# w_out and five more projections by seven products of quarters, and a first layer that begins in five parts

## The reference, cut to what matters

```
# first block, one layer (p: its weights)
shift, scale, gate = split(silu(c) @ p.w_ada + p.b_ada)      # same for ctx with c_ctx
h = x * (1 + scale) + shift                                  # ctx likewise
(a_q, a_k, a_v, a_g, g_q, g_k, g_v, g_af, g_ab, g_g,
 s_u, s_v, s_g, m_a, m_g, m_s) = split(h @ p.w_in)
y_attn = attention(a_q, a_k, a_v) * silu(a_g)
y_gla  = rms(gla scan, both directions) * silu(g_g)
y_sgu  = s_u * (w_s mixed over tokens of layer_norm(s_v) + b_s) * silu(s_g)
m   = sigmoid(m_a) * (y_attn @ w_br_attn) + sigmoid(m_g) * (y_gla @ w_br_gla) + sigmoid(m_s) * (y_sgu @ w_br_sgu)
x   = layer_norm(ALPHA * x + gate * (m @ w_out))             # ctx too, in the first layer only
# second block, one layer
h = rms(x) * norm_w ;  y = sigmoid(g0) * y_a + sigmoid(g1) * y_b ;  x = x + y @ w_out
# end
out = rms(x) * final_norm_w
```

## Time and profile before

| | us |
|---|---|
| median of three runs | 1534.58 |
| the profiled execution, whole | 1532.09 |
| its span (first to last instruction) | 1530.3 |
| PE busy | 1491.9 (97%) |
| DVE busy | 755.5 (49%) |
| ACT busy | 429.2 (28%) |
| POOL busy | 287.6 (19%) |

### The profile page before, as it was taken

The page is one execution under the profiler, slowest core; times in us unless marked ns, Lnnn a source line. Parts: engine busy times, 40 slices in busy tenths (PEclk is TensorE's granted clock), DMA queues, the critical chain, the costliest instruction groups (busy, mean ns, idle before and its releaser), DMA issues.

```text
span 1530.3 us, 20417 instructions
## 1 busy us (share of the span) xinstructions
PE 1491.9 (97%) x8416; PEld 1123.3 (73%) x8416; DVE 755.5 (49%) x1546; ACT 429.2 (28%) x846; POOL 287.6 (19%) x314
## 2 busy tenths in 40 slices
PE   6999999999999999999999999999999999999997
PEld 2577776554788884655977988588888858888883
DVE  1266656642634333533745631356887215679621
ACT  1132454323121220122336330134333213423310
POOL 0223203200566441122111202110100011010010
PEclk9999999999999999999999999999999999999999
DMA  9542224300122213421332352533232233232221
GB/s 370 225 165 111 111 110 166 135 31 20 63 96 106 100 57 102 152 110 55 110 111 110 111 221 110 195 115 121 111 112 106 109 150 145 110 129 99 105 110 42
DMA packets 17376, 184.31 MB, mean 120 GB/s; under 512 B 2306, under 2 KB 2818, under 8 KB 4740
## 3 DMA queue, kind: packets, MB, share of 16 engines
q1 hardware_dynamic: 17284, 183.01, 31.3%
HBM read 181.95 MB, written 1.05 MB: 120 GB/s over the span
## 4 chain that ended last, share of the span: by engine, by line
PE 89%; ACT 3%; DVE 3%; issue 2%; DMA 2%; POOL 1%; SPq 0%; POOLq 0%; ACTq 0%; DVEq 0%
PE ps L850 85%; PE ps L905 3%; DVE arena L1933 2%; DMA arena<-in_wf 2%; POOL arena L2607 1%; DVE arena L1927 0%; ACT L1887 0%; ACT L1885 0%; ACT arena L1459 0%; DVE arena L2134 0%; DVE arena L1930 0%; ACT arena L1885 0%; ACT arena L1771 0%; ACT L1773 0%; ACT L1771 0%
## 5 line engine op out<-in xcount | busy, mean ns | idle before, releaser
L850 PE MATMUL ps<-arena 128*128 128x256 f32 (+9 forms) x7924 | 1443.6, 365 | 28.1 <-DMA arena<-in_wf 13.5
L850 PEld LDWEIGHTS ps<-arena 128*128 128x128 f32 (+5 forms) x7924 | 1070.2, 178 | 368.7 <-issue 236.4
L2607 POOL TENSOR_TENSOR arena<-arena 128x256 f32<-128x256 f32 (+6 forms) x254 | 254.5, 1021 | 808.9 <-DVE arena L1933 374.2
L1933 DVE SCALAR_TENSOR_TENSOR arena<-arena 128x256 f32<-128x256 f32 (+4 forms) x482 | 237.8, 544 | 115.1 <-ACT arena L1486 21.2
L1459 ACT ACTIVATE arena<-ps 128x512 f32<-128x512 f32 (+3 forms) x312 | 148.9, 499 | 485.7 <-PE ps L850 410.6
L1927 DVE TENSOR_TENSOR arena<-arena 128x1024 f32<-128x1024 f32 (+12 forms) x253 | 205.8, 838 | 150.8 <-ACT arena L1459 83.2
L1927 DVE TENSOR_TENSOR arena<-ps,arena 128x512 f32<-128x512 f32 (+16 forms) x141 | 59.9, 449 | 123.8 <-PE ps L850 115.3
L1933 DVE SCALAR_TENSOR_TENSOR arena<-arena,ps 128x256 f32<-128x256 f32 (+2 forms) x109 | 47.2, 445 | 132.6 <-PE ps L850 90.7
L905 PEld LDWEIGHTS ps<-arena 128*128 128x128 f32 x488 | 55.8, 141 | 28.2 <-issue 18.3
L905 PE MATMUL ps<-arena 128*128 128x128 f32 x488 | 72.2, 278 | 1.3 <-DVE arena L1927 0.7
L1933 DVE SCALAR_TENSOR_TENSOR arena<-ps,arena 128x128 f32<-128x128 f32 (+2 forms) x86 | 30.8, 407 | 82.6 <-PE ps L850 82.2
(11 more groups left out here) (96 smaller groups left out, 308.2 us busy)
## 6 DMA issues: line engine op xcount, KB each, us to landing
arena<-in_wf SPq DMA_DIRECT2D x69, 2048.0 KB, 8.0
arena<-in_wf SPq DMA_DIRECT2D x22, 1024.0 KB, 7.8
arena<-in_wf SPq DMA_DIRECT2D x2, 1152.0 KB, 7.7
arena<-in_xinT SPq DMA_DIRECT2D x2, 1024.0 KB, 16.0
arena<-in_xin SPq DMA_DIRECT2D x4, 512.0 KB, 3.8
arena<-in_rp SPq DMA_DIRECT2D x2, 1024.0 KB, 8.4
arena<-in_consts SPq DMA_DIRECT2D x1, 1410.0 KB, 21.1
arena<-in_pa SPq DMA_DIRECT2D x2, 532.0 KB, 9.8
```

Of the source, the lines that this page charges most:

```text
L850: return e.matmul(o, l, r, start=start, stop=stop, skip_group_check=True)
L1933: return e.scalar_tensor_tensor(out=o, in0=x, scalar=s, in1=y, op0=op0, op1=op1)
L2607: return e.tensor_tensor(o, x, y, op)
```

## The change

- w_out of all four layers by seven products: four matmuls of 256 columns each, for a pair of token tiles and a half j of the outputs. A token tile is the stationary operand, the weight quarter moves. The two halves are interleaved (OUT_ORDER).
- VectorE makes the sums of w_out's weight quarters (8 of 128x1024 in each layer) during the last part of the merge, and the sums of the merged tokens (4 of 128x512 for each pair) after it. Product 1 of each half waits only for the first half of the features (`mg_add.at(l, 7)`, `mb_add.at(l, 3)`).
- sg and ma0 in both layers and mg1 in the second by seven products; sg now before su, and su is multiplied into the gated sg by VectorE (kind "M").
- Two buffers in turn (TM, TMB) for the addends of the merge, two for zz.
- The first layer begins in five parts: parts n carry k chunks (1, 1, 2, 2, 2) of shift and scale in one piece, and x transposed together with q's weights for those chunks; q is accumulated part by part. GpSimd makes no part of hT any more.
- The last norm is taken in quarters (squares) and halves (product and output).
- The order strings are other ones, and the pieces' places in the ring shift.

```diff
-ADA_FIRST = [(0, 0), (0, 2), (0, 1), (0, 3)]
+ADA_FIRST = [(0, 1), (1, 2), (2, 4), (4, 6), (6, 8)]
+OUT_PART = {1: (0, 0), 2: (0, 0), 6: (0, 1), 4: (0, 1), 7: (1, 1), 5: (1, 1), 3: (1, 0)}
+OUT_ORDER = [(0, 1), (0, 2), (0, 7), (0, 6), (1, 1), (0, 4), (1, 7), (1, 2), (1, 6), (1, 4), (0, 5), (1, 5), (0, 3), (1, 3)]
-SEVEN = [[("gqk", "A"), ("gv", "A"), ("ag", "T"), ("gg", "T"), ("su", "A")],
-         [("ag", "T"), ("gg", "T"), ("su", "A"), ("mg0", "G"), ("ms0", "G"), ("ma1", "G")]]
+SEVEN = [[("gqk", "A"), ("gv", "A"), ("ag", "T"), ("gg", "T"), ("sg", "T"), ("su", "M"), ("ma0", "G")],
+         [("ag", "T"), ("gg", "T"), ("sg", "T"), ("su", "M"), ("ma0", "G"), ("mg0", "G"), ("ms0", "G"), ("ma1", "G"),
+          ("mg1", "G")]]
-        short = [("a0gqk", "a0su"), ("a1ag", "a1ma1")]
+        short = [("a0gqk", "a0ma0"), ("a1ag", "a1mg1")]
-                    out[f"a{l}o{j}"] = ou_pe.at(l, NOUT[l] - 2 + j)
-                    out[f"b{l}o{j}"] = ob_pe.at(l, 2 + j)
+                    out[f"a{l}o{j}"] = a_out_made(l, len(PAIRS[l]) - 1, j, 4)
+                    out[f"b{l}o{j}"] = out_made(l, j, 4)
# SP, start
+            for n, (k0, k1) in enumerate(ADA_FIRST):
+                load(f"a0f{n}")
+                if n == 0:
+                    fetch(BADA[:, 0:24], pa[0][:, 0:24], d_bada)
+                    fetch(cst[:, C_ID:C_MASK], consts[:, C_ID:C_MASK], d_id)
+                fetch(FX[:, k0:k1, :], r3(first, 8)[:, k0:k1, :], d_first[n])
...
-            s.wait_ge(mg_dve.end(0), mg_add.end(0))
+            s.wait_ge(mg_pe.at(0, MGI[0][("m", "s", 1, 3)]))
# TensorE, start
-                    for n in range(2):
-                        ada_products(n, "pf", *ADA_FIRST[n])
...
+                    for n in range(len(ADA_FIRST)):
+                        first = (1, 2)[n == 2]
+                        for t in range(first if n else 0):
+                            first_queries(n - 1, t)
+                        ada_products(n, "pf", f"a0f{n}")
+                        for t in range(first, first + 1 if n else 0):
+                            first_queries(n - 1, t)
+                        ada_columns(n, "ps", "pf")
+                        for t in range(first + 1, 4 if n else 0):
+                            first_queries(n - 1, t)
# TensorE, w_out of layer_a (layer_b: out_product, the same with out_added, TO, WO)
-                p.wait_ge(mg_dve.end(l), mg_add.end(l))
-                for i, (t, hf) in enumerate((t, hf) for t in tiles(l) for hf in range(2)):
-                    token(bank("ou", l, i), use(f"a{l}o{hf}", 8), 512, mT, 128 * t).then_inc(ou_pe.hit(l, i), 1)
+                for pr in range(len(PAIRS[l])):
+                    for i, (j, x) in enumerate(OUT_ORDER):
+                        a_out_product(l, pr, j, x).then_inc(ou_pe.hit(l, 14 * pr + i), 1)
+            def a_out_product(l, pr, j, x):
+                ...
+                    b = psum("ou", l, pr, j, 7 if x == 4 else 1)
+                    p.wait_ge(a_out_taken(l, pr, j, {6: 1, 5: 6, 4: 7, 3: 5}[x]))
+                p.wait_ge(mg_add.at(l, 7) if x == 1 else mg_add.at(0, 14) if (l, pr, x) == (0, 0, 2) else mg_add.end(l))
+                ...
+                for k in range(4):
+                    ins = mm(b[:, 0:256], H[:, k, :], W[:, k, :], x in (1, 2, 7) and k == 0, k == 3)
# TensorE, layer_b
-                    if l == 0 and i == 3:
+                    if l == 0 and i == 13:
                         input_b(1, 0)
# ScalarE, layer_a
+                for pr in range(len(PAIRS[l])):
+                    for i, (j, x) in enumerate(BY_COPY):
+                        t, f = OUT_PART[x]
+                        a.wait_ge(a_out_made(l, pr, j, x), ln_x.at(l, t) if pr else None)
+                        o = SIG[1][:, 256 * j:256 * j + 256] if x == 7 else zz[t][:, 512 * j + 256 * f:512 * j + 256 * f + 256]
+                        copy(o, psum("ou", l, pr, j, 7 if x == 7 else 1)[:, 0:256]).then_inc(ou_act.hit(l, 8 * pr + i), 1)
# VectorE, layer_a: sums between the parts
+                            for _ in range((3, 3, 2, 0)[c] if l and (br, j) == ("s", 1) else 0):
+                                next(sums)
+                first = a_out_token_sums(l, 0)
+                next(first)
+                next(first)
+                sums = chain(first, sums, a_out_token_sums(l, 1) if l == 0 else ())
+                ...      # for each of OUT_ORDER: add, next(sums, None), after x in (4, 3) gated_half, after j = 1 normed
# VectorE, layer_b: a sum after each product of the last branch
-                for _ in merge(l, 1):
-                    pass
+                sums = out_weight_sums(l)
+                for n, _ in enumerate(merge(l, 1)):
+                    if n % 2:
+                        next(sums)
+            def out_weight_sums(l):
+                for j in range(2):
+                    w11, w12, w21, w22 = (quarter(weights(f"b{l}o{j}", 8), k, f) for f, k in ("11", "12", "21", "22"))
+                    v.wait_ge(pieces[f"b{l}o{j}"][2])
+                    tt(WO[j]["3"], w11, w21, ALU.subtract).then_inc(ob_w.hit(l, 4 * j), 1)
+                    yield
+                    ...      # 2 = w22 - 3, 1 = w21 + w22, 4 = w12 - 2
```

More of the change, by code:

```diff
@@ L1 @@
 from contextlib import ExitStack
+from itertools import chain
 import numpy as np
@@ L300, in build_program @@
         KDT = [attf[:, 0:512], attf[:, 512:1024]]
-        QB = [ma.take(512) for _ in range(2)]
+        qb = ma.take(1024)
+        QB = [qb[:, 0:512], qb[:, 512:1024]]
         ST = ma.take(1024).rearrange("p (d n v) -> p d n v", d=2, n=4)
@@ L2233, in later_piece @@
                     put(kind, 2, dst, 1, 1, MS_11 + o)
+                    if not o:
+                        next(sums, None)
+                        next(sums, None)
                     if o:
@@ new lines, in normed @@
+            def normed(l, pr, pair, t):
+                z, st, k, tile = zz[t], st6[:, 16 * t:16 * t + 16], pair[t] - tiles(l)[0], pair[t]
+                v.wait_ge(v.now())
+                e.bn_aggr(st[:, 12:14], r3(st[:, 0:12], 2)).then_inc(ln_st.hit(l, k), 1)
+                o = X[:, 1024 * t:1024 * t + 1024] if tile >= 2 else CX[:, 1024 * t:1024 * t + 1024]
+                v.wait_ge(ln_st.at(l, k), landed(d_rp, l))
+                stt(z, z, st[:, 12:13], rp[:, 0:1024], ALU.subtract, ALU.mult).then_inc(v.own(), 1)
+                v.wait_ge(v.now(), ln_rs.at(l, k))
+                stt(o, z, st[:, 14:15], rp[:, 1024:2048], ALU.mult, ALU.add).then_inc(ln_x.hit(l, k), 1)
@@ new lines, in layer_b @@
+                for n, _ in enumerate(merge(l, 1)):
+                    if n % 2:
+                        next(sums)
+                out_sums = out_token_sums(l)
+                next(out_sums)
+                next(out_sums)
+                for i, (j, x) in enumerate(OUT_ORDER):
+                    t, f = OUT_PART[x]
+                    o = X[:, 1024 * t + 512 * j + 256 * f:1024 * t + 512 * j + 256 * f + 256]
+                    v.wait_ge(ob_pe.at(l, i), out_added(l, j, {2: 1, 4: 6, 5: 7}[x]) if x in (2, 4, 5) else None)
+                    stt(o, psum("ou", 2 + l, j, {2: 2, 7: 7, 4: 7}.get(x, 1))[:, 0:256], 0.5, o, ALU.mult, ALU.add
+                        ).then_inc(ob_x.hit(l, i), 1)
+                    next(out_sums, None)
+                    if l and i in (10, 13):
+                        last_norm(i == 13)
@@ new lines, in last_norm @@
+            def last_norm(t):
+                ms = f2[:, 8 + t:9 + t]
+                v.wait_ge(fn_sq.at(1, 4 * t + 3))
+                e.tensor_reduce(ms, f2[:, 4 * t:4 * t + 4], AX, ALU.add).then_inc(v.own(), 1)
+                v.wait_ge(v.now())
+                ts(ms, ms, 1.0 / 1024, EPS, ALU.mult, ALU.add).then_inc(fn_ms.hit(1, t), 1)
+                v.wait_ge(fn_rs.at(1, t), landed(d_fr))
+                for hf in range(2):
+                    x = X[:, 1024 * t + 512 * hf:1024 * t + 512 * hf + 512]
+                    stt(x, x, ms, fr[:, 512 * hf:512 * hf + 512], ALU.mult, ALU.mult).then_inc(fn_x.hit(1, 2 * t + hf), 1)
@@ L2847 @@
     pieces = {}
+    for n, (a, b) in enumerate(ADA_FIRST):
+        w = I["w_ada"][0]
+        pieces[f"a0f{n}"] = lay(np.concatenate([w[:, o + 128 * a:o + 128 * b] for o in (0, 1024)], 1))
     for l in range(2):
```

518 lines of the change are left out of this document (319 added, 199 removed).

## The result

The changed kernel takes 1495.02 us, median of four runs (1493.66 to 1496.71), against 1534.36 (1532.9 to 1535.61; one run more than above): 0.975 of the time before, 95% interval 0.9735 to 0.9765. That is 39.3 us less where 33.7 was forecast (1501 from a range of 1493 to 1512). Measured again beside the first experiments it gave 1496.16 (1495.71 to 1497.12). The profiled execution took 1493.66, 38.4 less than the one before.

The account below looks back on a forecast made before the run. TensorE's work was taken as the bound, busy 1491.9 of 1530.3 us. Terms -28.2 -5.5 -5.4 +1.0 +3.3 -0.9 +2.0 = -33.7 gave a median of 1500.9, forecast 1501 us, range 1493 to 1512.

Parts of the forecast that it names:

- Products taken away: w_out, sg, ma0 and mg1 by seven products: fewer TensorE records, 28.2 us less.
- The start: Up to q's last copy: smaller parts let TensorE begin earlier, 5.5 us less, bounds 2 and 7.
- Seams from merge to w_out: Before each w_out: first product needs only half the features, covering the last addition; 5.4 of 5.8 us back.
- Inside w_out: First layer's w_out: TensorE waits for VectorE's late copy at the second pair, +1.0 us, bounds 0 and 4.
- Seam to the second block: Between the blocks: first token tile complete later and rp landing late, TensorE stands, +3.3 us, bounds 0 and 6.
- The end: After the last matmul: last norm in quarters and halves, write half as large, 0.9 us less.
- Added waits: Elsewhere, from four-unit ring loads and VectorE's added sums and gatings: +2.0 us, bounds -3 and +12.5.
- covers fail in the weave: Rival: sums of the five new pieces come late, 1511.5 us; chance 0.20 together with late w_out pieces.
- w_out's sums wait for their pieces: Rival: in both layers of the second block, 2 x 5 us, 1511; shares the 0.20 for covers or pieces late.
- The four-unit ring: Rival: first-layer loads each show for 8.0 us if attention and scan run out, 1549 us; chance 0.03.

Follow-up runs that it names:

- rp first: Changed kernel with the norm's rows (rp) fetched right after the merge's last addition, ahead of the second block's first load: 1494.68 us, ratio 0.975.
- the base: The changed kernel run again without edit, for comparison with the other runs: 1496.16 us, ratio 0.9759 to the kernel before.
- the two runs with the longer fillers: Changed kernel with unread matmuls at the seam to block two: eight, 1496.01 us; five, plus rp fetched first and product (1,1) second, 1494.30 us.
- the run that filled its gap with three matmuls: Changed kernel with rp fetched first, product (1,1) second and three unread matmuls at the seam to the second block: 1490.76 us, ratio 0.9726.

## Why the prediction was right

*Products taken away,* 28.2 forecast. By the page's groups the busy time went from 352.0 to 157.9 us in matmuls of 512 columns, from 799.4 to 926.0 in those of 256 and from 158.2 to 195.6 in those of 128: -30.1. The 592 records of 256 columns and the 336 of 128 that were added are 0.2139 and 0.1113 us each, as reckoned; the 448 of 512 columns that went are 0.433 each, with their tails, where 0.43 was used. In length w_out gave 5.9 + 0.5 of a new wait and 3.2, for 7.1 and 3.5. The runs with one w_out and with ma0 and mg1 by whole products confirm the price of products in place: 4.1 for 4.3, and in the first layer 3.7 for 3.7.

*The start,* 5.5: measured 5.2, with its one break; the run with four parts shows that TensorE and not the bytes sets it. That the half clock of the earlier trace rows did not come (0.97 over the stretch before, 1.00 after) was part of the gain. ("Bytes set it", as the prediction has it for the kernel before, holds no longer.)

*Seams from merge to w_out,* 5.4 of 5.8: 2.54, 0.54 and twice 1.36 became 0, 0 and twice 0.50, 4.8 back. What stayed is GpSimd's addition, 0.72 us before and 1.64 beside a weight sum, a lengthening that the prediction did not have. The run with one buffer shows that the rest hangs on the second buffer: the prediction counted the buffer in and never asked what it costs to be without it, which was the largest price of all.

*Inside w_out,* +1.0: 0.51, once.

*Seam to the second block,* +3.3: +4.2 of standing; rp landed 22.6 us into w_out (forecast 21.8) and VectorE waited 2.27 for it. On top come 0.6 to 2.8 us of the lower clock; 2.2 had been allowed for it.

*The end,* -0.9: from the last addition of w_out to the end of the span 7.5 became 5.9, -1.6.

*Added waits,* +2.0: this step failed. The stretches of the first block came out 2.4 and 1.3 below their terms. In the second block the body of the layers, where no term stood, got 1.4 and 2.6 shorter. But 1.7 of the 2.6 is no gain of the change: the kernel before has, in its profile, a stretch of low clock in that layer which the changed kernel's first profile lacks and its second has in the layer before (1160 to 1180).

```profile
1455.00:1460.00 5.00, 5.00 (x19) 4.13 (x19) 2.61 (x5) 2.26 (x4) 0.00 (x0) 0.77 0.00 0
```
And 0.85 of the 1.4 is a stand of the kernel before, at 1134.98, for nothing that the profile shows. Together with the end's 0.7, less 0.6 at the seams to w_out, 0.5 in the two w_outs and 0.6 of clock behind the seam, this gives about the 2.8 of the last row. The old strings in the changed kernel bring 8.2 and 1.5 back, so the strings, which I had taken for a mere consequence of the new pieces, matter; as no run has the new strings without the new pieces, how much of the missing gain they carry and how much went by chance is not shown. At an equal clock the change is 2 to 4 us better than the forecast, not 5.6, and the seams, which came out worse than forecast, hide part of what the weave gained.

Of the rivals, the first (covers fail in the weave) is in part what happens with the strings of the kernel before: 8.2 more, where I had put 12.5 at most, but only 4.2 of it as standing. That w_out's sums wait for their pieces did not happen even with the old strings. The four-unit ring showed in one wait of 0.31, as before in one of 1.01.

## What to carry to other kernels

A matmul taken away is worth its records, but only with what feeds it: without the second buffer the kernel is 12.0 us slower, with the old order of the first block 8.2, a third and a fifth of what the whole change brings. Where a stage ends in a norm, follow the chain to the next member before you price a fetch moved ahead, and look at the granted clock behind every stand. Count a filler in records before it goes in. Compare executions at an equal granted clock before a difference of 2 or 3 us is given a cause.

## What the hardware showed

**GpSimd beside VectorE.** An addition of 128x256 on GpSimd took 0.72 us in the kernel before. In the changed one eight of them take 13.71 us with the small gaps between them, 1.64 each without. Within one layer of the changed kernel both lengths stand, with a weight sum of VectorE beside the first addition and none beside the second:

```profile
930.11 1.64 POOL L2848 TENSOR_TENSOR arena<-arena 128x256 f32<-128x256 f32 x1 [3.54 <-DVE arena L2041]
...
935.29 0.73 POOL L2848 TENSOR_TENSOR arena<-arena 128x256 f32<-128x256 f32 x1 [3.54 <-DVE arena L2041]
```
The kernel before, and the changed one in the second block:

```profile
1215.47 0.72 POOL L2607 TENSOR_TENSOR arena<-arena 128x256 f32<-128x256 f32 x1 [106.06 <-DVE arena L1933]
```
```profile
1189.46 13.71 POOL L2848 TENSOR_TENSOR arena<-arena 128x256 f32<-128x256 f32 x8 [104.09 <-DVE arena L2041]
```
The Trainium skill ("SBUF — State Buffer", section "Who interferes with whom") says that a VectorE instruction with two inputs in SBUF contends with a GpSimd instruction that reads SBUF, over a shared pair of ports that it calls an exclusive lock. The trace agrees: with one buffer the sum runs from 1200.20 to 1201.42, the addition begins at 1200.37 and ends 0.59 us behind the sum, so that most of its own 0.72 comes after it; no gating runs meanwhile, the next begins at 1202.14. The same holds for an instruction of one column: GpSimd's first for the root took 0.29 us where VectorE stood for rp, and 1.39 in the run with rp first, beside VectorE's pass of 1.28.

**The clock after a stand.** TensorE came back at 1.2 GHz after standing 3.7 to 3.9 us (granted 0.50 to 0.52 from 965 to 970 in three profiles, 0.76 in the first), also after 2.6 (0.51, rp first), after 4.23 (0.71 and 0.58, one buffer) and after 1.94 (0.52, old strings of the first block); after 2.54 in the earlier trace rows it did not. The 80 matmuls behind the seam took between 0.6 and 2.8 us more than 9.20, different in each execution. At this seam the clock fell in all ten profiles of the changed kernel and its variants without fillers, and in none of the three with them. A low stretch also came behind three waits of 0.51 us for ScalarE, from 1455 to 1460 in the kernel before (0.77) and from 1165 to 1170 in the base (0.71), and in the two runs with the longer fillers; in all other layers and profiles the same three waits left the clock at 1.00. What decides between the two, no run here shows. The Trainium skill ("TensorE: Matmul & The Clock Gate", section "HAM oscillation — how this bites in real kernels") has gaps between bursts of matmuls bring the slow clock back; the seam agrees, and the run that filled its gap with three matmuls, at 1.00, shows it from the other side.
